# Seven products of squares in place of eight in six blocks of each down projection

## The chip, the cores and the metric

One core of one Trainium2 chip runs the whole program. The metric is the device time of that core in microseconds (us), from launch to end: 571.27 us, the median of 3 runs (571.06 to 572.11). The engines are TensorE (PE, its weight loads PEld), VectorE (DVE), ScalarE (ACT), GpSimd (POOL) and SyncE (SP), which here issues the loads.

## The reference

Two layers of a decoder trunk on 256 tokens of 1024 features, all in float32. Each layer has an attention part (two groups of eight heads, one input and one output projection) and a gated feed-forward part:

```
def hybrid_layer(x, ...):
    ...
    x = x + rms_norm(jnp.einsum('bse,ed->bsd', mix, w_out), g_attn_post)
    h = rms_norm(x, g_ffn_pre)
    f = jax.nn.silu(jnp.einsum('bsd,df->bsf', h, w_gate)) * jnp.einsum('bsd,df->bsf', h, w_up)
    x = x + rms_norm(jnp.einsum('bsf,fd->bsd', f, w_down), g_ffn_post)
```

The down projection `f @ w_down` multiplies 256 x 2816 by 2816 x 1024.

## The kernel before

The weights are cut on the host into blocks of 128 x 2048 float32 (1 MB); a layer has 46, of which the last 11 (`FIRST_DOWN` = 35 on) are the down projection, each 256 rows of `w_down` (two tiles of 128) by all 1024 columns. The tokens are two tiles, t = 0 and 1; a bank of PSUM holds 512 columns of one tile.

A float32 number is split into a high part, rounded to the type that TensorE multiplies, and a low part, the rest. Every product is three matmuls: high by high, high by low, low by high. So a block takes 24 matmuls of 128 x 128 by 128 x 512: two token tiles, eight products of squares (four to a tile), three matmuls each.

A block's way is the same for all. SyncE loads it into one of three slots of `raw` (`load_block`). ScalarE makes the high part `w_h` (`hi`, L559) as soon as the block before it in its slot of `w` (four slots) has been used, VectorE the low part `w_l` (`lo`, L812), and TensorE multiplies (`multiply`, L1209). `freed_by(b)` lists the blocks that may be split once block b has been used; ScalarE and VectorE call `after(L, b)` at places written out by hand, and each engine does its work in exactly that order. A raw slot is loaded again when its low part is done.

The feed-forward part goes by chunks c of 512 of the 2816 inner features (six; the last has 256). Of each chunk and tile ScalarE computes the SiLU of the gate (L671), VectorE multiplies by the up projection (`swiglu`, L1002) and transposes within squares of 32 (`squares_f`, L1013), and GpSimd moves the squares between partitions with 16 copies of 32 partitions (`exchange`, L517): then the features lie along the partitions. ScalarE and VectorE split the result into `fT_h` (`hi_f`, L594) and `fT_l` (`lo_f`, L1020). The chunk's parts are the left operands of the down projection: chunk c feeds the blocks of k = 4c to 4c + 3. GpSimd does this exchange for all six chunks in order, and besides it only sums and powers of one column for the norms (L479 to L505).

TensorE multiplies the first seven down blocks for both tiles, then the last four for tile 0, then for tile 1, with the transposes of the next layer's tile 0 (L1249) put in among the last.

## Time and profile before

| | |
|---|---|
| median of 3 runs | 571.27 us (571.06 to 572.11) |
| profiled execution: span from first to last instruction | 569.7 us |
| between that span and the median of the runs | 1.6 us |
| TensorE busy | 562.0 us, 99% |
| VectorE, ScalarE, GpSimd busy | 375.1, 294.0, 229.1 us |
| read from HBM | 105.72 MB, 187 GB/s over the span |

The profile gives no time of its own for the profiled execution besides its span; the 1.6 us around it are launch and end as the runs' times have them. Busy time of an engine is the time in which it had an instruction under way, and matmuls overlap, so the duration of one (about 390 ns) is longer than the distance from one to the next.

### The profile page before, as it was taken

The numbers are of one execution on the slowest core, as the hardware profiler recorded it, in microseconds if no ns is written. First come the engines' busy times: TensorE is split into PE (matmuls) and PEld (weight loads), VectorE is DVE, ScalarE is ACT, GpSimd is POOL, SyncE is SP. The second block draws the span as 40 slices with busy tenths as digits, with TensorE's granted clock in tenths as the row PEclk, the third lists the DMA queues.
The fourth block names the chain that finished last, engine by engine and source line by source line (L and its number), as shares of the span: only waits on it lengthen the run. The fifth ranks groups of instructions, "written<-read, shape, count | busy, mean of one in ns | idle before, by whom it ended". The sixth has DMA issues, their size and how long they took to land.

```text
span 569.7 us, 8885 instructions
## 1 busy us (share of the span) xinstructions
PE 562.0 (99%) x3395; PEld 462.1 (81%) x3395; DVE 375.1 (66%) x487; ACT 294.0 (52%) x420; POOL 229.1 (40%) x451
## 2 busy tenths in 40 slices
PE   8999999999999999999999999999999999999996
PEld 5878878888888888888888878888888888888884
DVE  5799895946755746365597987775855746734622
ACT  6576684664445353263546748574645354425420
POOL 1101001507797797860120000033296797785000
PEclk9999999999999999999999999999999999999999
DMA  8954624538556461478266443525575455352701
GB/s 299 370 210 156 237 89 173 223 133 315 184 217 202 167 221 33 189 294 298 89 239 208 158 167 124 211 76 221 222 258 201 173 217 183 113 221 88 282 1 74
DMA packets 18730, 107.34 MB, mean 188 GB/s; under 512 B 2816, under 2 KB 3072, under 8 KB 7168
## 3 DMA queue, kind: packets, MB, share of 16 engines
q1 hardware_dynamic: 18688, 106.78, 50.8%
q8 instruction: 27, 0.44, 0.3%
q14 instruction: 15, 0.12, 0.1%
HBM read 105.72 MB, written 1.05 MB: 187 GB/s over the span
## 4 chain that ended last, share of the span: by engine, by line
PE 93%; DVE 3%; DMA 1%; ACT 1%; issue 1%; POOL 0%; SPq 0%; DVEq 0%; POOLq 0%
PE bank L1209 84%; PE bank L1249 4%; PE bank L1234 2%; PE bank L1275 2%; PE bank L1302 2%; DVE w_l L812 1%; DMA raw<-in_w_blocks 1%; ACT work L631 0%; DVE work L896 0%; DVE work L874 0%; DVE work L897 0%; DVE work L952 0%; DVE work L902 0%; DVE x L986 0%; ACT work L608 0%
## 5 line engine op out<-in xcount | busy, mean ns | idle before, releaser
L812 DVE TENSOR_TENSOR w_l<-raw,w_h 128x2048 fp32r<-128x2048 f32 x90 | 206.6, 2301 | 112.6 <-ACT w_h L559 112.4
L559 ACT ACTIVATE w_h<-raw 128x2048 fp32r<-128x2048 f32 x90 | 171.7, 1915 | 108.5 <-PE bank L1209 91.5
L1209 PE MATMUL bank<-w_h,actT_h 128*128 128x512 f32 (+1 forms) x568 | 223.9, 394 | 0.1
L517 POOL COPY work<-work 32x128 f32<-32x128 f32 (+1 forms) x384 | 191.3, 498 | 75.6 <-DVE work L1013 59.8
L1209 PE MATMUL bank<-w_h,actT_l 128*128 128x512 f32 (+1 forms) x568 | 219.9, 387 | 0.0
L1209 PE MATMUL bank<-w_l,actT_h 128*128 128x512 f32 (+1 forms) x568 | 219.4, 386 | 0.0
L1209 PEld LDWEIGHTS bank<-w_h,actT_h 128*128 128x128 f32 x568 | 106.8, 188 | 23.1 <-issue 2.5
L1209 PEld LDWEIGHTS bank<-w_h,actT_l 128*128 128x128 f32 x568 | 106.7, 188 | 22.1
L1209 PEld LDWEIGHTS bank<-w_l,actT_h 128*128 128x128 f32 x568 | 106.9, 188 | 20.1
L504 POOL TENSOR_TENSOR norms<-norms,constants 128x1 f32<-128x1 f32 x8 | 2.7, 342 | 131.7 <-ACT bank L658 131.7
L1209 PE MATMUL bank<-w_h,fT_h 128*128 128x512 f32 x160 | 49.4, 390 | 0.0
L1209 PE MATMUL bank<-w_l,fT_h 128*128 128x512 f32 x160 | 49.3, 389 | 0.0
L1209 PE MATMUL bank<-w_h,fT_l 128*128 128x512 f32 x160 | 49.2, 389 | 0.0
L487 POOL TENSOR_TENSOR norms<-norms,constants 128x1 f32<-128x1 f32 x8 | 6.2, 771 | 72.6 <-ACT work L608 72.6
L1209 PEld LDWEIGHTS bank<-w_l,fT_h 128*128 128x128 f32 x160 | 30.0, 188 | 6.3
L1209 PEld LDWEIGHTS bank<-w_h,fT_l 128*128 128x128 f32 x160 | 30.0, 188 | 6.2
L1209 PEld LDWEIGHTS bank<-w_h,fT_h 128*128 128x128 f32 x160 | 30.0, 188 | 6.2
L1249 PE MATMUL bank<-ident,work 128*128 128x128 f32 x228 | 31.3, 273 | 0.0
L631 ACT ACTIVATE work<-bank,neg_max 128x128 f32<-128x128 f32 (+1 forms) x64 | 26.0, 429 | 10.0 <-DVE neg_max L922 9.9
L1249 PEld LDWEIGHTS bank<-ident,work 128*128 128x128 f32 x228 | 26.9, 140 | 4.7
L671 ACT ACTIVATE work<-bank,norms 128x512 f32<-128x512 f32 (+1 forms) x24 | 15.7, 653 | 28.2 <-PE bank L1209 28.2
L594 ACT ACTIVATE fT_h<-work 128x512 fp32r<-128x512 f32 x20 | 12.5, 624 | 34.3 <-POOL work L517 34.3
(78 smaller groups left out, 396.1 us busy)
## 6 DMA issues: line engine op xcount, KB each, us to landing
raw<-in_w_blocks SPq DMA_DIRECT2D x90, 1024.0 KB, 4.8
bias<-in_b_in SPq DMA_DIRECT2D x8, 256.0 KB, 6.1
raw<-in_w_blocks SPq DMA_DIRECT2D x4, 256.0 KB, 5.9
raw<-in_w_blocks SPq DMA_DIRECT2D x2, 512.0 KB, 8.6
x<-in_x SPq DMA_DIRECT2D x2, 512.0 KB, 10.7
gain_b<-in_g_attn_post SPq DMA_DIRECT2D x2, 512.0 KB, 7.3
bias<-in_g_ffn_pre SPq DMA_DIRECT2D x2, 512.0 KB, 7.4
...
```

The costliest lines, as they stand in the source:

```text
L487: add = nc.gpsimd.tensor_tensor(ss_y[:, t, 0:1], ss_y[:, t, 0:1], eps, ALU.add)
L517: ins = nc.gpsimd.tensor_copy(crossed[t][32 * j:32 * j + 32, i * n:(i + 1) * n], squares[t][32 * i:32 * i + 32, j * n:(j + 1) * n])
L559: nc.scalar.activation(w["h"][:, slot(b), :], raw[:, r, :], ACT.Copy).then_inc(hi_ready, 1)
L594: nc.scalar.activation(f_part("h", c, t), f_view(c, t), ACT.Copy).then_inc(f_hi_ready, 1)
L631: last = nc.scalar.activation(probs[g, r][:, j, n * keys:(n + 1) * keys], bank[b][:, n * keys:(n + 1) * keys], ACT.Exp, bias=neg_max[:, g, ...
L671: nc.scalar.activation(silu[t][:, 0:n], bank[b][:, 0:n], ACT.Silu, scale=rstd_x[:, t:t + 1]).then_inc(drained[b] if c < LAST else last_sil ...
L812: nc.vector.tensor_tensor(w["l"][:, slot(b), :], raw[:, slot(b, RAW), :], w["h"][:, slot(b), :].bitcast(F32), ALU.subtract).then_inc(lo_re ...
L1209: ins = nc.tensor.matmul(bank[BANK_OF[name]][:, 0:n], left[s][:, at + k, tokens(t)], right[r][:, k, c * BANK:c * BANK + n], start=first an ...
L1234: ins = nc.tensor.matmul(bank[BANK_OF[name]][:, 0:n], actT[s][:, k, tokens(t)], right[r][:, k, :], start=first, stop=last and (s, r) == pr ...
L1249: ins = nc.tensor.transpose(out_[:, q * P:(q + 1) * P], src(q), ident[:])
L1275: ins = nc.tensor.matmul(bank[b][:, n * keys:(n + 1) * keys], qT[g][side, i, tokens(t)], kT[g][side, i if g == MOBA else 0, 0:keys], start ...
L1302: ins = nc.tensor.matmul(bank[b][rows, h * HEAD:(h + 1) * HEAD], probsT[g, r][:, j, at + side * 32:at + (side + 1) * 32], v[g][:, kb, cols ...
```

## The change

In six of the eleven down blocks (k = 0 to 11) the 2 x 2 squares of the left operand (two token tiles by two feature tiles, a11 to a22) and of the weights (b11 to b22) are multiplied by a form of Strassen's scheme: seven products in place of eight, each of three matmuls as before. Four products use sums of left squares (s1 to s4), four use sums of weight squares (t1 to t4). VectorE makes the s from the exchanged features, once for each of the first three chunks (`add_s`), and the two engines split them (`hi_s`, `lo_s`). GpSimd makes the t from the raw block with three instructions of 1024, 512 and 512 columns (`add_squares`). A square is thus two entries in the list of blocks: "raw", of which three quarters are split and used, and "sum", split from GpSimd's result and not loaded. Four PSUM banks hold products (M1, M6, M5, M7), and VectorE combines them into the four output banks (`join_first`, `join_second`) with eight additions of 512 columns, in part before TensorE adds the last blocks to the same banks.

The order changes with it: block k = 12 first, then the six squares, then k = 14, 16, 18, 20. GpSimd does the exchange of chunks 4 and 5 after the six sums, where it did them directly after chunk 3 before. The slot order is new (the place at which the raw slots skip is load 26, not block 38), and several buffers share memory.

```diff
@@ -56,9 +56,21 @@
 BLOCKS += [("both", k, 4, LAST * BANK, BANK) for k in (0, 4)]
 FIRST_DOWN = len(BLOCKS)
 KF = FF // P
...
+FAST = 6
+FAST_CHUNKS = FAST // 2
+BLOCKS += [("down", 2 * FAST, 2, 0, D)]
+for k in range(0, 2 * FAST, 2):
+    BLOCKS += [("raw", k, 2, 0, D), ("sum", k, 2, 0, D)]
+BLOCKS += [("down", k, 2, 0, D) for k in range(2 * FAST + 2, KF, 2)]
 NB = len(BLOCKS)
+FIRST_RAW = FIRST_DOWN + 1
+FIRST_LATE = FIRST_RAW + 2 * FAST
+LOADED = [b for b in range(NB) if BLOCKS[b][0] != "sum"]
+NL = len(LOADED)
 PROJ_COLS = [(4 * GROUP, 256), (3 * GROUP, BANK), (GROUP, BANK), (0, BANK), (2 * GROUP, BANK)]
...
+def slot(b):
+    return b % SLOTS
+def before(b):
+    return b - SLOTS
+def raw_slot(b):
+    n = LOADED.index(b)
+    return n % RAW if n < SKIP_AT else (n - NL) % RAW
+def raw_before(b):
+    n = LOADED.index(b) - 1
+    while raw_slot(LOADED[n]) != raw_slot(b):
+        n -= 1
+    return LOADED[n]
...
+        sums_own = sb("sums_own", [P, 2, 2 * BANK])
+        fX = {s: sb("fX_" + s, [P, 10, P], F32R) for s in "hl"}
+        sums = [sums_own[:], gains[:].rearrange("p (a n) -> p a n", a=2),
+                work_row[:, 0:4 * BANK].rearrange("p (a n) -> p a n", a=2)]
+        m1_sum = rope_tmp
+        u4, u2, u3, u7 = (work[:, q, :] for q in (0, 2, 3, 2))
+        s_raw = work_row[:, 0:2 * BANK].rearrange("p (s k n) -> p s k n", s=4, k=2)
         ident = sb("ident", [P, P])
         masks = sb("masks", [P, 4, P], BF16)
...
-                    place_free(lo_ready, L * NB + before(b, RAW) + 1)
-                sp.dma_start(raw[:, r, :], w_blocks[L, b]).then_inc(raw_in[r], 16)
+                    past_L, past = (L, raw_before(b)) if raw_before(b) < b else (L - 1, raw_before(b))
+                    place_free(lo_ready, past_L * NB + past + 1)
+                    if BLOCKS[past][0] == "raw":
+                        place_free(sums_ready, sums_done(past_L, BLOCKS[past][1] // 2))
+                sp.dma_start(raw[:, r, :], w_blocks[L, LOADED.index(b)]).then_inc(raw_in[r], 16)
...
+            def add_squares(L, n):
+                b = FIRST_RAW + 2 * n
+                r = raw_slot(b)
+                dst = sums_of(n)
+                b12, b11, b22, b21 = (raw[:, r, q * BANK:(q + 1) * BANK] for q in range(4))
+                pool.wait_ge(raw_in[r], RAW_IN[r].done(L, b) * 16)
+                if n >= SUMS:
+                    pool.wait_ge(lo_ready, L * NB + b + 2 - 2 * SUMS)
+                if n == 2:
+                    pool.wait_ge(s_lo_ready, FAST_CHUNKS * (L + 1))
+                    pool.wait_ge(drained[BANK_OF["both", LAST, 1]],
+                                 HELD[BANK_OF["both", LAST, 1]].done(L, ("both", LAST, 1)) + 1)
+                nc.gpsimd.tensor_tensor(dst[:, 0, :].rearrange("p (a n) -> p a n", a=2),
+                                        raw[:, r, BANK:3 * BANK].rearrange("p (a n) -> p a n", a=2),
+                                        b12.unsqueeze(1).broadcast_to([P, 2, BANK]), ALU.subtract
+                                        ).then_inc(sums_step, 1)
+                pool.wait_ge(sums_step, 2 * (L * FAST + n) + 1)
+                nc.gpsimd.tensor_tensor(dst[:, 1, 0:BANK], dst[:, 0, BANK:2 * BANK], b11, ALU.add).then_inc(sums_step, 1)
+                pool.wait_ge(sums_step, 2 * (L * FAST + n) + 2)
+                nc.gpsimd.tensor_tensor(dst[:, 1, BANK:2 * BANK], b21, dst[:, 1, 0:BANK], ALU.subtract
+                                        ).then_inc(sums_ready, 1)
...
+                    for t in range(T):
+                        exchange(L, c, t)
+                pool.wait_ge(crossed_in[T - 1], f_count(L, FFN_CHUNKS - 3))
+                for n in range(FAST):
+                    add_squares(L, n)
+                    pool.wait_ge(sums_ready, sums_done(L, n))
+                for c in (FFN_CHUNKS - 2, FFN_CHUNKS - 1):
                     for t in range(T):
                         exchange(L, c, t)
                 rms_y(L, 1, 0)
...
                     act.wait_ge(block_used, USED.done(L, last % NB) + (USED.n if last >= 0 else 0))
-                nc.scalar.activation(w["h"][:, slot(b), :], raw[:, r, :], ACT.Copy).then_inc(hi_ready, 1)
+                if m == "sum":
+                    nc.scalar.activation(w["h"][:, slot(b), :].rearrange("p (a n) -> p a n", a=2), sums_of(k0 // 2),
+                                         ACT.Copy).then_inc(hi_ready, 1)
+                else:
+                    at = BANK if m == "raw" else 0
+                    nc.scalar.activation(w["h"][:, slot(b), at:], raw[:, r, at:], ACT.Copy).then_inc(hi_ready, 1)
             def hi_early(b, p):
...
+            def hi_s(L, c):
+                act.wait_ge(s_added, FAST_CHUNKS * L + c + 1)
+                nc.scalar.activation(s_tiles("h", c), s_raw.rearrange("p s k n -> p (s k) n"), ACT.Copy
+                                     ).then_inc(s_hi_ready, 1)
+            def keep_m1(L):
+                act.wait_ge(block_used, USED.done(L, FIRST_LATE - 2) + USED.n)
+                nc.scalar.activation(m1_sum, products[0][:], ACT.Copy).then_inc(m1_kept, 1)
...
@@ -771,14 +901,18 @@
                         after(L, b + 2)
                         hi_f(L, c - 1, 0)
                         hi_f(L, c - 1, 1)
+                        if c <= FAST_CHUNKS:
+                            hi_s(L, c - 1)
                         after(L, b + 3)
-                hi_f(L, FFN_CHUNKS - 2, 0)
+                for b in range(FIRST_DOWN, NB - 4):
+                    if b == FIRST_LATE - 2:
+                        keep_m1(L)
+                    after(L, b)
+                    if b == NB - 8:
+                        hi_f(L, FFN_CHUNKS - 2, 0)
                 hi_f(L, FFN_CHUNKS - 2, 1)
-                for b in range(FIRST_DOWN, NB - 4):
-                    after(L, b)
-                    if b == FIRST_DOWN + 4:
-                        hi_f(L, FFN_CHUNKS - 1, 0)
-                        hi_f(L, FFN_CHUNKS - 1, 1)
+                hi_f(L, FFN_CHUNKS - 1, 0)
+                hi_f(L, FFN_CHUNKS - 1, 1)
                 sum_y(L, 1, 0)
                 if L < depth - 1:
                     hi(L + 1, 0)
...
-                nc.vector.tensor_tensor(w["l"][:, slot(b), :], raw[:, slot(b, RAW), :],
-                                        w["h"][:, slot(b), :].bitcast(F32), ALU.subtract).then_inc(lo_ready, 1)
+                m, k0 = BLOCKS[b][0:2]
+                if m == "sum":
+                    low, high = (w[s][:, slot(b), :].rearrange("p (a n) -> p a n", a=2) for s in "lh")
+                    nc.vector.tensor_tensor(low, sums_of(k0 // 2), high.bitcast(F32), ALU.subtract
+                                            ).then_inc(lo_ready, 1)
+                else:
+                    at = BANK if m == "raw" else 0
+                    nc.vector.tensor_tensor(w["l"][:, slot(b), at:], raw[:, raw_slot(b), at:],
+                                            w["h"][:, slot(b), at:].bitcast(F32), ALU.subtract).then_inc(lo_ready, 1)
             def after(L, b):
                 for c in freed_by(b):
...
+            def add_s(L, c):
+                for t in range(T):
+                    dve.wait_ge(crossed_in[t], f_count(L, c))
+                if L or c:
...
+                s1, s3, s2, s4 = (s_raw[:, q].rearrange("p k (i b) -> p k i b", b=32) for q in range(4))
+                a11, a12 = f_odd(c, 0, 0), f_odd(c, 0, 1)
+                a21, a22 = f_odd(c, 1, 0), f_odd(c, 1, 1)
+                nc.vector.tensor_tensor(s3, a11, a21, ALU.subtract)
+                link(L, nc.vector.tensor_tensor(s1, a21, a22, ALU.add))
+                link(L, nc.vector.tensor_tensor(s2, s1, a11, ALU.subtract))
+                nc.vector.tensor_tensor(s4, a12, s2, ALU.subtract).then_inc(s_added, 1)
+            def lo_s(L, c):
+                dve.wait_ge(s_hi_ready, FAST_CHUNKS * L + c + 1)
+                nc.vector.tensor_tensor(s_tiles("l", c), s_raw.rearrange("p s k n -> p (s k) n"),
+                                        s_tiles("h", c).bitcast(F32), ALU.subtract).then_inc(s_lo_ready, 1)
+            def join(L, t, c, what):
+                x = bank[BANK_OF["down", t, c]]
+                nc.vector.tensor_tensor(x[:], x[:], what, ALU.add).then_inc(joined, 1)
+            def join_first(L):
...
+                _, m6, m5, _ = products
+                dve.wait_ge(m1_kept, L + 1)
+                join(L, 0, 0, m1_sum)
+                dve.wait_ge(products_full, 3 * L + 1)
+                link(L, nc.vector.tensor_tensor(u2, m1_sum, m6[:], ALU.add))
+                dve.wait_ge(products_full, 3 * L + 2)
+                link(L, nc.vector.tensor_tensor(u4, u2, m5[:], ALU.subtract))
+                join(L, 0, 1, u4)
+            def join_second(L):
+                _, _, m5, m7 = products
+                dve.wait_ge(products_full, 3 * L + 3)
+                link(L, nc.vector.tensor_tensor(u3, u2, m7[:], ALU.add))
+                dve.wait_ge(second_begun, L + 1)
+                join(L, 1, 0, u3)
+                link(L, nc.vector.tensor_tensor(u7, u3, m5[:], ALU.subtract))
+                join(L, 1, 1, u7)
             nc.vector.memset(still, 0.0).then_inc(still_ready, 1)
             dve.wait_ge(xT_in_done[0], 16)
@@ -1125,6 +1312,8 @@
                     for q in range(b + 1, end):
                         after(L, q)
                     if c < FFN_CHUNKS - 1:
+                        if c <= FAST_CHUNKS:
+                            add_s(L, c - 1)
                         lo_f(L, c - 1, 0)
                         lo_f(L, c - 1, 1)
                     swiglu(L, c, 0)
@@ -1134,14 +1323,21 @@
                     after(L, end)
                     if c < FFN_CHUNKS - 1:
                         squares_f(L, c, 1)
-                for t in range(T):
-                    lo_f(L, FFN_CHUNKS - 2, t)
-                    squares_f(L, FFN_CHUNKS - 1, t)
-                for b in range(FIRST_DOWN, NB - 4):
+                    if c <= FAST_CHUNKS:
+                        lo_s(L, c - 1)
+                for b in range(FIRST_DOWN, NB - 7):
                     after(L, b)
-                    if b == FIRST_DOWN + 4:
-                        lo_f(L, FFN_CHUNKS - 1, 0)
-                        lo_f(L, FFN_CHUNKS - 1, 1)
+                lo_f(L, FFN_CHUNKS - 2, 0)
+                squares_f(L, FFN_CHUNKS - 1, 0)
+                join_first(L)
+                after(L, NB - 7)
+                after(L, NB - 6)
+                lo_f(L, FFN_CHUNKS - 2, 1)
+                squares_f(L, FFN_CHUNKS - 1, 1)
+                after(L, NB - 5)
+                lo_f(L, FFN_CHUNKS - 1, 0)
+                join_second(L)
+                lo_f(L, FFN_CHUNKS - 1, 1)
                 scale_y(L, 1, 0)
                 update_x(L, 1, 0)
                 if L < depth - 1:
...
+            def product(out_, left, right, first, last):
+                for s, r in (("h", "h"), ("h", "l"), ("l", "h")):
+                    ins = nc.tensor.matmul(out_[:], left[s], right[r], start=first and (s, r) == ("h", "h"),
+                                           stop=last and (s, r) == ("l", "h"))
+                return ins
+            def squares(L, n):
+                c, k = n // 2, n % 2
+                b = FIRST_RAW + 2 * n
+                first, last = n == 0, n == FAST - 1
+                m1, m6, m5, m7 = products
+                x11, x12, x21 = (bank[BANK_OF["down", t, q]] for t, q in ((0, 0), (0, 1), (1, 0)))
+                a11, a12 = ({s: f_tiles(s, c, 0)[:, 2 * k + u, :] for s in "hl"} for u in range(2))
+                a22 = {s: f_tiles(s, c, 1)[:, k, :] for s in "hl"}
+                s1, s3, s2, s4 = ({s: s_tiles(s, c)[:, 2 * q + k, :] for s in "hl"} for q in range(4))
+                b11, b22, b21 = ({s: w[s][:, slot(b), q * BANK:(q + 1) * BANK] for s in "hl"} for q in range(1, 4))
+                t1, t3, t2, t4 = ({s: w[s][:, slot(b + 1), q * BANK:(q + 1) * BANK] for s in "hl"} for q in range(4))
+                pe.wait_ge(f_lo_ready, F_PARTS.done(L, (c, 1)))
+                pe.wait_ge(s_lo_ready, FAST_CHUNKS * L + c + 1)
+                pe.wait_ge(lo_ready, L * NB + b + 1)
+                product(m1, a11, b11, first, last)
+                product(x12, s4, b22, False, last)
+                product(x11, a12, b21, False, last).then_inc(block_used, 1)
+                USED.tick(b)
+                pe.wait_ge(lo_ready, L * NB + b + 2)
+                ends = [product(m6, s2, t2, first, last), product(m5, s1, t1, first, last),
+                        product(m7, s3, t3, first, last)]
+                if last:
+                    for ins in ends:
+                        ins.then_inc(products_full, 1)
+                product(x21, a22, t4, False, last).then_inc(block_used, 1)
+                USED.tick(b + 1)
             def early(b, t, p, *products, last=False):
...
-                f_landed(L, FFN_CHUNKS - 3)
-                for b in range(FIRST_DOWN, NB - 4):
-                    multiply(L, 0, b)
-                    multiply(L, 1, b)
-                f_landed(L, FFN_CHUNKS - 1)
-                for b in range(NB - 4, NB):
-                    multiply(L, 0, b)
-                for b in range(NB - 4, NB):
-                    if b == NB - 2:
-                        if L < depth - 1:
-                            rows(L + 1, 0, 0)
-                    multiply(L, 1, b)
+                f_landed(L, FFN_CHUNKS - 3, T - 1)
+                multiply(L, 0, FIRST_DOWN)
+                multiply(L, 1, FIRST_DOWN)
+                for n in range(FAST):
+                    squares(L, n)
+                multiply(L, 1, FIRST_LATE, (0,), asks=True).then_inc(second_begun, 1)
+                multiply(L, 0, FIRST_LATE, asks=False, apart=True)
+                f_landed(L, FFN_CHUNKS - 2, 0)
+                multiply(L, 0, FIRST_LATE + 1)
+                multiply(L, 0, FIRST_LATE + 2)
+                f_landed(L, FFN_CHUNKS - 1, 0)
+                multiply(L, 0, FIRST_LATE + 3)
+                pe.wait_ge(joined, 4 * L + 4)
+                multiply(L, 1, FIRST_LATE, (1,))
+                multiply(L, 1, FIRST_LATE + 1)
+                multiply(L, 1, FIRST_LATE + 2, (0,))
+                if L < depth - 1:
+                    rows(L + 1, 0, 0)
+                multiply(L, 1, FIRST_LATE + 2, (1,))
+                f_landed(L, FFN_CHUNKS - 1, 1)
+                multiply(L, 1, FIRST_LATE + 3)
```

`f_tiles` and `s_tiles` say where the split features and their sums lie; `USED`, `LOADED` and the semaphores count as before.

## Rows read from the trace of the kernel before

**Rows 1.** The page's busy line and its clock line, 40 slices.
```profile
PE 562.0 (99%) x3395; PEld 462.1 (81%) x3395; DVE 375.1 (66%) x487; ACT 294.0 (52%) x420; POOL 229.1 (40%) x451
PEclk9999999999999999999999999999999999999999
```

**Rows 2.** The chain that ended last: start, length, what.
```profile
114.64 165.94 PE bank L1209 x732
...
392.83 170.03 PE bank L1209 x750
```

**Rows 3.** Line L1209: durations, first and last start.
```profile
L1209 PEld LDWEIGHTS bank<-w_h,fT_h x160: 187/188/192, 225.8 to 560.0; 128*128 128x128 f32 x160
```

**Rows 4.** Groups by line: busy, mean ns of one.
```profile
L812 DVE TENSOR_TENSOR w_l<-raw,w_h 128x2048 fp32r<-128x2048 f32 x90 | 206.6, 2301 | 112.6 <-ACT w_h L559 112.4
...
L559 ACT ACTIVATE w_h<-raw 128x2048 fp32r<-128x2048 f32 x90 | 171.7, 1915 | 108.5 <-PE bank L1209 91.5 <-DMA raw<-in_w_blocks 17.1
...
L1020 DVE TENSOR_TENSOR fT_l<-work,fT_h 128x512 fp32r<-128x512 f32 x20 | 14.5, 725 | 18.6 <-ACT fT_h L594 18.6
...
L594 ACT ACTIVATE fT_h<-work 128x512 fp32r<-128x512 f32 x20 | 12.5, 624 | 34.3 <-POOL work L517 34.3
```

**Rows 5.** GpSimd's copies: line L517, then its timeline, idle time in brackets.
```profile
L517 POOL COPY work<-work x384: 226/287/2433, 130.7 to 521.9; 32x128 f32<-32x128 f32 x160, 32x64 f32<-32x64 f32 x32
...
197.41 18.95 POOL L517 COPY work<-work 32x128 f32<-32x128 f32 x32 [3.39 <-DVE work L1013]
...
274.58 0.19 POOL L487 TENSOR_TENSOR norms<-norms,constants 128x1 f32<-128x1 f32 x1 [22.82 <-ACT work L608]
...
479.47 13.12 POOL L517 COPY work<-work 32x128 f32<-32x128 f32 x22
```

**Rows 6.** Busy time in stretches; the last row GpSimd's copies alone.
```profile
core 0: us, PE busy (x) PEld busy (x) DVE busy (x) ACT busy (x) POOL busy (x), PEclk, DMA share, GB/s
241.50:244.50 3.00, 3.00 (x15) 2.49 (x14) 0.00 (x0) 1.91 (x2) 2.52 (x11) 1.00 0.63 205
246.00:251.00 5.00, 5.00 (x24) 4.14 (x23) 5.00 (x3) 2.13 (x2) 4.92 (x3) 1.00 0.52 203
...
226.00:229.50 3.50, 3.07 (x11) 1.00 0.97 321
```

**Rows 7.** GpSimd's one-column instructions, and VectorE beside them: line L479, then timelines.
```profile
L479 POOL TENSOR_TENSOR norms<-norms,constants x8: 190/1259/2247, 19.8 to 389.7; 128x1 f32<-128x1 f32 x8
...
111.50 2.25 POOL L479 TENSOR_TENSOR norms<-norms,constants 128x1 f32<-128x1 f32 x1 [3.10 <-ACT work L599]
...
111.42 2.29 DVE L812 TENSOR_TENSOR w_l<-raw,w_h 128x2048 fp32r<-128x2048 f32 x1
...
280.99 1.26 POOL L479 TENSOR_TENSOR norms<-norms,constants 128x1 f32<-128x1 f32 x1 [4.16 <-ACT work L599]
282.32 0.55 POOL L481 TENSOR_TENSOR norms<-norms,constants 128x1 f32<-128x1 f32 x1
...
279.90 2.29 DVE L812 TENSOR_TENSOR w_l<-raw,w_h 128x2048 fp32r<-128x2048 f32 x1 [0.43 <-ACT w_h L559]
282.11 1.28 DVE L842 TENSOR_TENSOR actT_l<-bank,actT_h 128x512 fp32r<-128x512 f32 x2
```

**Rows 8.** VectorE's timeline from chunk 3 into the down projection.
```profile
179.26 2.39 DVE L812 TENSOR_TENSOR w_l<-raw,w_h 128x2048 fp32r<-128x2048 f32 x1 [1.25 <-ACT w_h L559]
...
194.72 0.69 DVE L1020 TENSOR_TENSOR fT_l<-work,fT_h 128x512 fp32r<-128x512 f32 x1 [1.52 <-ACT fT_h L594]
...
201.02 2.29 DVE L812 TENSOR_TENSOR w_l<-raw,w_h 128x2048 fp32r<-128x2048 f32 x1 [0.88 <-ACT w_h L559]
...
211.90 2.29 DVE L812 TENSOR_TENSOR w_l<-raw,w_h 128x2048 fp32r<-128x2048 f32 x1 [2.63 <-ACT w_h L559]
...
244.54 6.85 DVE L812 TENSOR_TENSOR w_l<-raw,w_h 128x2048 fp32r<-128x2048 f32 x3 [3.15 <-ACT w_h L559]
```

**Rows 9.** DMA issues: out<-in, KB each, us to landing.
```profile
raw<-in_w_blocks SPq DMA_DIRECT2D x90, 1024.0 KB, 4.8
```

142 lines of the change are left out of this document (89 added, 53 removed).

## Prediction

> **What bounds the kernel now.** I read the page's busy line and clock first, then the chain of waits, then the engines' timelines around the first down projection, then the rows in which GpSimd and VectorE run at once. TensorE is busy for 562.0 of 569.7 us at the full granted clock [rows 1], and the chain of waits is the matmuls of L1209 nearly throughout. Two pieces of it hold both feed-forward parts: 165.94 us for 732 matmuls and 170.03 us for 750, so 0.2267 us each and no wait between [rows 2]. The durations of 0.39 us in the groups are pipelined and are no price. The down projection of layer 0 starts at 225.8 [rows 3]. A block of 24 matmuls is 24 x 0.2267 = 5.44 us; beside it ScalarE makes one high part (1.915 us) and VectorE one low part (2.30 us) [rows 4], so both have slack.
>
> The resource that matters here shows elsewhere. GpSimd's 32x64 copy takes 0.226 us at the shortest, and in the same group one takes 2.433 [rows 5]. From 246 to 251 us VectorE is busy all 5.00 us with low parts and GpSimd completes 3 copies in that time; in 241.5 to 244.5, with VectorE idle, it does 11 in 3 us [rows 6]. It is no matter of copies: the TENSOR_TENSOR of L479 on one column takes 0.190 us at best, but 2.25 when it starts at 111.50 beside a low part of 111.42 (2.29), and 1.26 at 280.99, ending with the low part that began at 279.90 [rows 7]. L481 at 282.32 keeps its 0.55 us beside L842 of 282.11, one of whose inputs is in PSUM [rows 7]. So a VectorE instruction with two SBUF inputs keeps GpSimd out until it ends.
>
> **What the change takes away.** Six blocks take 7 products of 3 matmuls in place of 8: 21 x 0.2267 = 4.76 us, 0.68 less. Six blocks, two layers: 36 matmuls, -8.16 us, -4.08 a layer. That is all the gain there can be.
>
> **What it adds, per square.** VectorE: low part of 1536 columns, and of 2048 for the sums. From 512 columns at 0.69 to 0.73 and 2048 at 2.29 [rows 4, 8] a column costs 1.04 ns: 1.76 + 2.29 = 4.05 us in place of 2.29. ScalarE the same way: 1.48 + 1.92 = 3.40; both would fit in 4.76 by themselves. GpSimd: three sums of 1024, 512 and 512 columns, which no row shows. Its copies give 0.17 us of launch and 0.95 ns a column (0.226 for 64 columns, 3.07/11 = 0.28 to 0.287, the median, for 128) [rows 5, 6]. Lower bound: a sum costs what a copy does, 3 x 0.17 + 2048 x 0.95 ns = 2.45 us. Upper bound: two operands and the result each take the copy's time, 6.35 us. I take two operands read one after the other, 4.4 us, since a copy differs from a sum by one operand more.
>
> The rows show only that VectorE keeps GpSimd out. I take it both ways, because something that one engine holds to the end of its instruction is most plainly a lock, and so the two times add up: 4.4 + 4.05 = 8.45 us a square, less 0.45 for three launches that run while the other engine moves data (short copies slip between three low parts, 6.85 us in all, without lengthening them [rows 8]). 8.0 us against TensorE's 4.76: the sums become the bound, 3.24 us a square over.
>
> The Trainium skill (GPSIMD Engine Reference, section on performance versus the Vector engine) gives 4497 ns for one add of 2048 fp32 columns; with two launches more my sum by that price would be some 619 us. No run here shows it.
>
> **How far ahead GpSimd is.** It can begin when the exchange of chunk 3 ends, 216.4 now (197.41 + 18.95) [rows 5]. VectorE gets four additions of 256 columns (about 0.43 each) and a low part of 1024 (1.22) per early chunk, all with two SBUF inputs: near 3 us, which also lock out that chunk's copies. TensorE does not feel them: low parts are finished 11.6 us ahead (that of the block multiplied from 225.8 ended at 214.2 [rows 8]). But chunk 3's exchange ends later, at about 221.8. The first sum is then ready near 226.7, its low part near 232.4, and TensorE wants it at 225.8 + 5.44 + 2.04 = 233.3: the first square passes. Three low parts fall into the second sum (1.76, 2.29 and 1.76, less overlap), so it is ready near 236.1 and, with its high part (1.92) and low part (2.29), usable at 240.4; TensorE wants it at 236.0 + 2.04: 2.4 us late. The next four follow at 8.0 us, 3.2 to 3.3 late each. Together 15.5 us; the sixth sum is ready at 236.1 + 4 x 8.0 = 268.1, and TensorE ends the squares at 275.3.
>
> The loads are no cause: a raw block lands 4.8 us after issue [rows 9] and is wanted once in 8 us. It is now also held by the sums, which come before the next load is due.
>
> **What is queued behind.** The exchanges of chunks 4 and 5, which were done at 251.8 (274.58 less 22.82 of idle time, [rows 5]), well ahead of the blocks that need them, now stand behind the sixth sum. The 16 copies of (4,0) are 5.1 us alone and wait for two low parts: 277.2. ScalarE's copy of M1 stands behind the high part of that chunk and one more block, and VectorE's first join behind that: 277.2 + 0.7 + 1.9 + 0.6 + 0.7 = 281.2 with the handovers, while TensorE, done with half a late block at 276.7, waits 4.5 us. The second join (two PSUM additions of 0.7) costs 0.8, the low part behind it 0.9. (5,0) follows (4,1) and waits for three low parts; it ends at 293.3 and is split by 294.3, with TensorE there at 291.1: 3.2. The last joins 0.2. Together 9.7 us. The joins themselves read PSUM, lock nobody out, and else lie under TensorE's four late blocks.
>
> Sum: 15.5 + 9.7 - 4.1 = +21.1 us a layer, and the same in the other layer, where chunk 3's exchange (ended 492.6 [rows 5]) is 10.4 us ahead of the down projection (264 matmuls before 562.86 [rows 2], 503.0), against 9.4 here. +42.2. The smaller buffers, slots moved from block 38 to 26 and the renamed regions I cost at nothing: a load that now waits for the neighbouring block's low part still leaves 11.6 + 5.4 - 4.8 - 1.9 - 2.3 = 8 us. The queue to the next layer is unchanged but for 18 matmuls instead of 24 behind the transposes, 1.4 us of cover less, which the new pace of low parts hides. Made against the profiled span of 569.7, with 1.6 us around it to the median of 571.3: **613.5 us**.
>
> **Rivals.**
> *Only GpSimd waits.* It waits to start while VectorE's instruction runs, but once it has the data path a long sum does not hold VectorE. Rows cannot exclude it: copies are too short, and low parts beside them read 2.29 and 2.39 [rows 8]. Then a square takes about 7.1 us (4.4 and what is left of a low part at each of three starts); the tail stays. +15.1 a layer, 601.5; at copy price +5.6, 582.5. The Trainium skill (SBUF — State Buffer, section on who interferes with whom) says the other: an exclusive lock for whoever starts first, "the other **fully blocks**". The rows agree in one direction; by that rule the forecast stands.
> *Sums at the copy's price*, both waiting: 2.45 + 4.05 is still over 4.76. Squares lose little (about 5 us), the exchanges still come late: +10.5 a layer, 592.3.
> *Sums at the upper price*: 32.8 a layer, 637. Gaps of 3 to 5 us in TensorE's work might also bring its lower clock, which this trace never shows after the start; that would end near here too.
> *Faster.* The sums run beside the low parts. It decides at one place: whether GpSimd's three sums end within 4.76 us while VectorE works 4.05 of them. For it: GpSimd is idle for 22.8 us from 251.8 on [rows 5], and TensorE has not waited once in the part. If sums of [128 x 512] share the memory path as single columns do not, TensorE waits only for joins, 0.4 us a layer: -3.7, that is 563.9. Against it stand all of rows 6 and 7.
> A change that does less than it says is excluded by the count of products, 21 in the code of a square.
>
> **Chances.** Forecast 0.48; only GpSimd waits 0.17; copy price 0.10; upper price or clock 0.10; faster 0.13; within 0.2% 0.02, by a cancellation nobody can plan. 0.2% (1.1 us) is about what a measurement of this kernel tells from no change. Range 578 to 632: it takes in the forecast with the larger part of the way to the upper price, the one-sided wait at both prices and the copy's price (582.5 the lowest); faster (0.13) and the upper price itself stay out. Slower 0.85.
>
> **What would show it.** TensorE idle before the sums' half of each square from the second on, released by VectorE's low part, which waited for ScalarE, which waited for GpSimd. GpSimd's first sum (1024 columns) near 2.1 us alone and 3 or more beside a low part; low parts of 2048 columns stretched beyond 2.29 where a sum had begun (not so if only GpSimd waits). A wait of 4 to 5 us before the first joined bank, one of 3 before the last block of tile 0. Wrong if the low parts and the sums lie side by side at 2.29 and 2 us with TensorE unbroken, or if GpSimd's rows for 512 columns are under 0.5 us.

## The result: 627.3 us, slower by a tenth

The changed kernel takes 627.33 us (median of 4 runs, 626.9 to 629.22) beside 571.16 for the kernel before in the same session: a ratio of 1.0987, interval 1.097 to 1.1005. The forecast was 613.5, slower; the time lies in its range, 14 us above its middle.

First the page of the changed kernel: the busy line, the clock line, and the chain that ended last, by engine.

```profile
PE 572.4 (92%) x3359; PEld 463.9 (74%) x3359; DVE 448.1 (72%) x545; ACT 315.3 (50%) x440; POOL 336.3 (54%) x487
...
PEclk9999999999999978988899999999999999699889
...
POOL 46%; PE 36%; DVE 9%; issue 5%; ACT 2%; DVEq 0%; POOLq 0%; ACTq 0%
```

The chain went by TensorE nearly throughout [rows 2]; now GpSimd has 46% of it. The span is 625.2 against 569.7: +55.5. TensorE runs 36 instructions fewer and is busy 10.4 us longer than in [rows 1]; its idle time grew from 7.7 to 52.8 us. Part of the added busy time is a lower clock: the clock line, flat in [rows 1], now dips several times in each of the two down projections.

GpSimd's timeline in the first down projection (start, length, what; L614, L619 and L621 are the three sums of a square, L597 the exchange's copies; the sums are named by the buffer that they go to, `sums_own`, `gains` and `work` in turn):

```profile
222.56 2.41 POOL L614 TENSOR_TENSOR sums_own<-raw 128x1024 f32<-128x1024 f32 x1
...
226.72 1.26 POOL L621 TENSOR_TENSOR sums_own<-raw,sums_own 128x512 f32<-128x512 f32 x1
228.06 3.75 POOL L614 TENSOR_TENSOR gains<-raw 128x1024 f32<-128x1024 f32 x1
231.89 3.19 POOL L619 TENSOR_TENSOR gains<-gains,raw 128x512 f32<-128x512 f32 x1
235.16 2.68 POOL L621 TENSOR_TENSOR gains<-raw,gains 128x512 f32<-128x512 f32 x1
237.92 2.40 POOL L614 TENSOR_TENSOR work<-raw 128x1024 f32<-128x1024 f32 x1
240.39 1.29 POOL L619 TENSOR_TENSOR work<-work,raw 128x512 f32<-128x512 f32 x1
241.76 1.30 POOL L621 TENSOR_TENSOR work<-raw,work 128x512 f32<-128x512 f32 x1
...
269.31 2.67 POOL L621 TENSOR_TENSOR work<-raw,work 128x512 f32<-128x512 f32 x1
272.04 28.09 POOL L597 COPY work<-work 32x128 f32<-32x128 f32 x56
```

VectorE's timeline beside it (L953 the low part of a raw block, L949 that of a sum block, L1143 `swiglu`):

```profile
227.38 2.21 DVE L953 TENSOR_TENSOR w_l<-raw,w_h 128x1536 fp32r<-128x1536 f32 x1
...
230.15 3.81 DVE L949 TENSOR_TENSOR w_l<-sums_own,w_h 128x2048 fp32r<-128x2048 f32 x1
233.88 0.86 DVE L1143 SCALAR_TENSOR_TENSOR work<-bank,norms,work 128x256 f32<-128x256 f32 x2
234.67 2.03 DVE L953 TENSOR_TENSOR w_l<-raw,w_h 128x1536 fp32r<-128x1536 f32 x1
243.94 3.75 DVE L949 TENSOR_TENSOR w_l<-gains,w_h 128x2048 fp32r<-128x2048 f32 x1 [7.24 <-ACT w_h L674]
...
253.68 3.95 DVE L953 TENSOR_TENSOR w_l<-raw,w_h 128x1536 fp32r<-128x1536 f32 x1
...
273.96 2.29 DVE L949 TENSOR_TENSOR w_l<-work,w_h 128x2048 fp32r<-128x2048 f32 x1 [3.11 <-ACT w_h L674]
```

Read the two together, by their ends. GpSimd's sum of 3.75 us begins at 228.06. VectorE's low part before it ends at 229.59, and from there the sum takes 2.22. VectorE's low part of 3.81 begins at 230.15; that sum ends at 231.81, and from there the low part takes 2.15. GpSimd's 3.19 begins at 231.89 and ends 1.12 after that low part. Each takes about its own length from the moment at which the other ends, by turns and in both directions. The lengths alone are about 2.41, 1.27 and 1.27 us for the three sums (2.40, 1.29 and 1.30 from 237.92 on, where VectorE is idle) and 2.29 for the low part (273.96, where GpSimd's short copies run, and [rows 4]).

TensorE's timeline, the matmuls ahead of which it was idle (in brackets: how long, and what ended it), with one matmul of lower clock (269.17):

```profile
234.61 1.19 PE L1408 MATMUL bank<-w_h,fT_h 128*128 128x512 f32 x2 [9.03 <-DVE work L1143]
...
253.81 0.50 PE L1423 MATMUL bank<-w_h,fT_h 128*128 128x512 f32 x1 [0.35 <-DVE w_l L949]
...
257.77 0.47 PE L1423 MATMUL bank<-w_h,fT_h 128*128 128x512 f32 x1 [0.94 <-DVE w_l L953]
...
260.97 0.50 PE L1423 MATMUL bank<-w_h,fT_h 128*128 128x512 f32 x1 [0.91 <-DVE w_l L949]
...
268.14 0.50 PE L1423 MATMUL bank<-w_h,fX_h 128*128 128x512 f32 x1 [2.03 <-DVE w_l L949]
...
269.17 0.63 PE L1423 MATMUL bank<-w_h,fX_h 128*128 128x512 f32 x1
...
276.31 0.50 PE L1423 MATMUL bank<-w_h,fX_h 128*128 128x512 f32 x1 [1.50 <-DVE w_l L949]
...
285.06 0.50 PE L1408 MATMUL bank<-w_h,fT_h 128*128 128x512 f32 x1 [4.38 <-DVE bank L1187]
...
298.74 0.50 PE L1408 MATMUL bank<-w_h,actT_h 128*128 128x512 f32 x1 [3.60 <-DVE actT_l L1161]
...
324.19 0.50 PE L1408 MATMUL bank<-w_h,actT_h 128*128 128x512 f32 x1 [1.04 <-DVE w_l L953]
```

Up to 298.74 that is 22.7 us of waits; the forecast had 25.2, otherwise placed. One it did not have at all: 9.03 us ahead of the first down block. That block adds into the banks of the last chunk's gate and up, and `swiglu`, which empties them (L1143), stands on VectorE behind the low part of 3.81. Two I had: 4.38 for the first join (forecast 4.5) and 3.60 for chunk 5's features (3.2). The sign that I had named, a wait ahead of the sums' half of each square from the second on, shows from the third square on, with 0.35, 0.91, 2.03 and 1.50 us. Layer 0 as a whole is 28.2 us longer, measured at the next layer's first attention scores (307.82 before, 335.99 after), the second layer 27.3.

### The profile page after: what moved, and what is told of

The parts are those of the page before. It is cut to its first block, busy times and chain, and to the rows that moved or that the text cites. A ratio compares the mean times of both kernels' runs of the same rounds, so it can differ in the third digit from the quotient of the medians.

```text
span 625.2 us, 8989 instructions
## 1 busy us (share of the span) xinstructions
PE 572.4 (92%) x3359; PEld 463.9 (74%) x3359; DVE 448.1 (72%) x545; ACT 315.3 (50%) x440; POOL 336.3 (54%) x487
## 4 chain that ended last, share of the span: by engine, by line
POOL 46%; PE 36%; DVE 9%; issue 5%; ACT 2%; DVEq 0%; POOLq 0%; ACTq 0%
POOL work L597 31%; PE bank L1408 27%; PE bank L1485 3%; POOL gains L614 3%; DVE w_l L953 2%; PE bank L1470 2%; POOL work L614 2%; POOL gains L621 2%; POOL gains L619 2%; PE bank L1511 2%; PE bank L1538 2%; POOL sums_own L614 2%; POOL sums_own L619 2%; DVE work L1143 1%; POOL work L619 1%
## 5 line engine op out<-in xcount | busy, mean ns | idle before, releaser
L953 DVE TENSOR_TENSOR w_l<-raw,w_h 128x2048 fp32r<-128x2048 f32 (+1 forms) x90 | 213.0, 2372 | 55.5 <-ACT w_h L678 54.8
L1408 PE MATMUL bank<-w_h,actT_h 128*128 128x512 f32 (+1 forms) x600 | 235.3, 396 | 7.7 <-DVE actT_l L1161 6.7
L597 POOL COPY work<-work 32x128 f32<-32x128 f32 (+1 forms) x384 | 200.9, 523 | 76.9 <-DVE work L1154 60.9
L1408 PE MATMUL bank<-w_h,actT_l 128*128 128x512 f32 (+1 forms) x600 | 231.2, 390 | 0.0
L1408 PE MATMUL bank<-w_l,actT_h 128*128 128x512 f32 (+1 forms) x600 | 230.6, 389 | 0.0
L678 ACT ACTIVATE w_h<-raw 128x2048 fp32r<-128x2048 f32 (+1 forms) x90 | 165.9, 1855 | 54.6 <-PE bank L1408 35.0
L1408 PEld LDWEIGHTS bank<-w_h,fT_h 128*128 128x128 f32 x32 | 7.9, 254 | 30.1 <-issue 18.6
L949 DVE TENSOR_TENSOR w_l<-gains,w_h 128x2048 fp32r<-128x2048 f32 x4 | 15.4, 3840 | 15.4 <-ACT w_h L674 15.4
L1423 PE MATMUL bank<-w_l,fT_h 128*128 128x512 f32 x64 | 25.0, 391 | 0.0
L1423 PE MATMUL bank<-w_h,fT_l 128*128 128x512 f32 x64 | 25.0, 390 | 0.0
```

What stands on the lines that cost most here:

```text
L597: ins = nc.gpsimd.tensor_copy(crossed[t][32 * j:32 * j + 32, i * n:(i + 1) * n], squares[t][32 * i:32 * i + 32, j * n:(j + 1) * n])
L678: nc.scalar.activation(w["h"][:, slot(b), at:], raw[:, r, at:], ACT.Copy).then_inc(hi_ready, 1)
L949: nc.vector.tensor_tensor(low, sums_of(k0 // 2), high.bitcast(F32), ALU.subtract).then_inc(lo_ready, 1)
L953: nc.vector.tensor_tensor(w["l"][:, slot(b), at:], raw[:, raw_slot(b), at:], w["h"][:, slot(b), at:].bitcast(F32), ALU.subtract).then_inc( ...
L1408: ins = nc.tensor.matmul(bank[BANK_OF[name]][:, 0:n], left[s][:, k, :], right[r][:, k, c * BANK:c * BANK + n], start=first and k == 0 and ...
L1423: ins = nc.tensor.matmul(out_[:], left[s], right[r], start=first and (s, r) == ("h", "h"), stop=last and (s, r) == ("l", "h"))
```

## The experiments

My theory after this: the sums and the low parts exclude each other, and this is the larger part; the late exchanges cost the next; and the 9.03 us are slack, which the sums would have cost anyway. Rivals: the sums are slow in themselves, the banks' wait is on the path, or the lower clock is. Several of these kernels leave out work or put other values in its place, so their output is not the product; each expectation says what.

**Without the sums (no_sums).**

```diff
-                nc.gpsimd.tensor_tensor(dst[:, 1, 0:BANK], dst[:, 0, BANK:2 * BANK], b11, ALU.add).then_inc(sums_step, 1)
...
+                nc.gpsimd.tensor_tensor(junk_sum, eps, minus_half, ALU.add).then_inc(sums_ready, 1)
```

> GpSimd's three sums of a square become one sum of one column; the splits of the 'sum' blocks read the raw block instead of the sums, so the output is not the product (the second operand of four products is wrong) and all other work, its sizes and its order are kept. Theory (the data path shared by GpSimd and VectorE is the bound; the sums fill it): about 40 us vanish, near 585 us; low parts back at 2.29 and 1.76 us, TensorE waits no more inside the squares, and what is left over the kernel before is the wait for the gate products ahead of the first down block and the late exchanges. Rival (the joins, the extra splits and the new order cost most of the 56 us by themselves): above 605 us.

599.33 us (597.84 to 600.82), ratio 1.0487 (1.0455 to 1.0519). Without the sums 28 of the 56 us go; I had expected some 14 us more. In its trace TensorE still waits 5.55 us for the banks of the last chunk, then 2.03 and 3.63 in the tail. That the banks' wait is no longer slack once the sums are gone is tried further down (no_sums_gate_first).

**Low parts that take one input from PSUM (psum_lows).** If the exclusion needs two SBUF inputs, this takes it away in the squares and leaves both engines their work. M7 is added into M5's bank, to free the one that is read, and a sum block's low part becomes two instructions of 1024 columns.

```diff
-                    nc.vector.tensor_tensor(w["l"][:, slot(b), at:], raw[:, raw_slot(b), at:],
-                                            w["h"][:, slot(b), at:].bitcast(F32), ALU.subtract).then_inc(lo_ready, 1)
+                        nc.vector.tensor_tensor(three(w["l"][:, slot(b), at:]), three(raw[:, raw_slot(b), at:]),
+                                                bank[7][:].unsqueeze(1).broadcast_to([P, 3, BANK]), ALU.subtract
+                                                ).then_inc(lo_ready, 1)
```

> GpSimd's sums stay at full size; the low parts of the 'raw' and 'sum' blocks subtract a PSUM bank (broadcast) in place of the high part in SBUF, so VectorE does the same number of columns with only one SBUF input. The values of those low parts are wrong; M5 and M7 share a bank, which frees the one that is read. Theory (exclusion because of two SBUF inputs): the sums go side by side with the low parts, 2.4 + 1.3 + 1.3 = 5.0 us a square, near TensorE's 4.76, and the time falls to about 581 us. Rival (GpSimd's sums are slow by themselves, and VectorE's part in it is small): no more than 10 us are won, above 615 us.

594.82 us (594.47 to 595.16), ratio 1.0408 (1.0387 to 1.0429): 32.5 us less than the changed kernel. GpSimd's timeline of this kernel over the same stretch:

```profile
229.17 2.37 POOL L614 TENSOR_TENSOR gains<-raw 128x1024 f32<-128x1024 f32 x1
231.62 1.28 POOL L619 TENSOR_TENSOR gains<-gains,raw 128x512 f32<-128x512 f32 x1
232.98 1.27 POOL L621 TENSOR_TENSOR gains<-raw,gains 128x512 f32<-128x512 f32 x1
```

and VectorE's:

```profile
231.07 2.35 DVE L950 TENSOR_TENSOR w_l<-sums_own,bank 128x1024 fp32r<-128x1024 f32 x2 [0.25 <-ACT w_h L674]
...
234.12 1.74 DVE L962 TENSOR_TENSOR w_l<-raw,bank 128x1536 fp32r<-128x1536 f32 x1
```

Side by side nothing here is stretched: 2.37 and 2.35 (both halves of the low part together) where it was 3.75 and 3.81. That the sums are slow in themselves (above 615) falls. The 32.5 us are not the sums' alone: this kernel is 4.5 us faster than the one without sums, and the 64 late copies take 28.23 us (from 258.46 on) where they take 33.60 there (from 254.44 on). I had expected some 14 us less than came out. In what is left, 23 us, TensorE waits 7.48 us ahead of the first down block and 3.01 for chunk 5's features, and nowhere within layer 0's squares.

**The gate's work ahead of the squares (gate_first).** The low and high parts of the first square go behind the last chunk's SiLUs and `swiglu`.

```diff
-                    after(L, b)
+                    if c < FFN_CHUNKS - 1:
+                        after(L, b)
...
+                    if c == FFN_CHUNKS - 1:
+                        after(L, b)
```

> ScalarE and VectorE do the gate of the last chunk before they split the first sum block, so the two banks that the first down block writes are free about 5 us earlier; nothing else changes. Theory (the sums on the shared path set the end of the squares, and TensorE's 9 us wait ahead of the down projection is slack behind them): the time stays within 2 us of the changed kernel's 627.3, at most 3 to 5 us less if the lower granted clock (0.59 from 226 to 236 us) cost anything; the wait moves into the squares. Rival (that wait is a cost of its own, the term that my sum lacked): 9 us less in each layer, near 610 us.

627.15 us (626.99 to 628.12), ratio 1.0979 (1.096 to 1.0997): no gain. Three of TensorE's waits in it:

```profile
231.03 1.16 PE L1414 MATMUL bank<-w_h,fT_h 128*128 128x512 f32 x2 [5.00 <-DVE work L1146]
...
259.84 0.50 PE L1429 MATMUL bank<-w_h,fT_h 128*128 128x512 f32 x1 [3.35 <-DVE w_l L952]
...
268.35 0.59 PE L1429 MATMUL bank<-w_h,fX_h 128*128 128x512 f32 x1 [3.35 <-DVE w_l L952]
```

The first wait shrinks by 4.0 us, and 3.9 us come back at the squares: their waits are now 1.42, 3.35, 3.35 and 1.49, in sum 9.6 against 5.7. Two of them are what the forecast had for each (3.2 to 3.3). The sixth square's sum half begins at 276.51 against 276.31: the sums set it. So 4 us of the largest wait in the trace were worth nothing; the 5.00 that stay were not tried by themselves.

**One copy in place of sixteen for the late exchanges (one_copy_late).**

```diff
+                        if c >= FFN_CHUNKS - 2 and (i, j) != (3, 3):
+                            continue
```

> The exchanges of chunks 4 and 5 do one copy in place of 16 (most of these features are not exchanged, so the output is wrong); the sums and all else stay. Theory (these exchanges, queued behind the sixth sum, cost what my sum gave the tail, 9.7 us a layer less the joins, which stay): 14 to 20 us less than 627.3, near 611 us. Rival (the exchanges are hidden behind the sums' delay of TensorE): within 4 us of the changed kernel.

607.04 us (606.54 to 607.55), ratio 1.0622 (1.0601 to 1.0643): 20.3 us back, at the top of what I had expected. The squares' waits stand (2.03 and 1.48 for the last two), those of 4.38 and 3.60 are gone, and one of 0.63 for a late block's low part comes in. The late copies, with the lower clock that follows their waits, cost some 10 us a layer.

**The first join ahead of the features (join_early).** On ScalarE the high part of chunk 4's first features moves back behind the copy of M1, on VectorE its low part behind the joins.

```diff
-                    if b == NB - 8:
+                    if b == FIRST_LATE - 2:
                         hi_f(L, FFN_CHUNKS - 2, 0)
...
                 for b in range(FIRST_DOWN, NB - 7):
                     after(L, b)
+                join_first(L)
                 lo_f(L, FFN_CHUNKS - 2, 0)
                 squares_f(L, FFN_CHUNKS - 1, 0)
-                join_first(L)
```

> ScalarE's copy of M1 goes ahead of the high part of chunk 4's features, and VectorE's first joins ahead of its low part; all work stays. Theory (TensorE's 4.4 us before the first joined bank is order, not work: the copy and the join stand behind an exchange that they do not need): that wait goes, the next one (chunk 4's features) takes half of it back; with the 3.4 us at half clock that follow each of these waits, 4 to 8 us less than 627.3, near 621 us. Rival (the sixth sum and the exchanges behind it set the end whatever is put ahead of them): within 1.5 us of 627.3, since the exchange of (5,0) ends at the same time.

628.56 us (627.86 to 629.41), ratio 1.1001 (1.0982 to 1.1019): the theory (near 621) fell, its rival (within 1.5 us) stood. TensorE's waits of the tail:

```profile
286.06 0.70 PE L1408 MATMUL bank<-w_h,actT_h 128*128 128x512 f32 x2 [2.09 <-DVE w_l L953]
...
299.34 0.80 PE L1408 MATMUL bank<-w_h,actT_h 128*128 128x512 f32 x1 [7.56 <-DVE actT_l L1161]
```

The wait of 4.38 for the join is gone; one of 2.09 for a late block's low part comes in, and 3.60 becomes 7.56. Chunk 5's features let TensorE go on at 299.34 against 298.74 (this trace is already 0.55 later at the first down block), wherever the joins stand: GpSimd's copies of chunk 5's first tile queue behind those of chunk 4 and between the low parts.

**The sums on VectorE (sums_on_vector).** Sums and low parts then stand in one queue and cannot exclude each other. GpSimd is free for the exchanges directly after chunk 3 again, though VectorE's transposes of chunk 5 still come late.

```diff
-                for n in range(FAST):
-                    add_squares(L, n)
-                    pool.wait_ge(sums_ready, sums_done(L, n))
...
             def lo(L, b):
...
+                if m == "raw":
+                    add_squares(L, k0 // 2)
```

> VectorE makes the weight sums itself, just ahead of the low part of the same raw block; GpSimd goes on with the exchanges. Theory (one shared path, used by whoever works): a square costs VectorE 1.76 + 2.29 + 2.3 + launches = 6.7 us instead of 8.25 us on the shared path, still over 4.76: near 600 us, 25 us less than the changed kernel and far slower than before. Rival (GpSimd's rate alone was at fault): VectorE's own sums at half the price would bring it near 575 us.

604.35 us (603.23 to 605.46), ratio 1.0572 (1.0545 to 1.0599), near the 600 of the theory and far from the rival's 575. VectorE's timeline, one square:

```profile
243.37 2.35 DVE L948 TENSOR_TENSOR w_l<-gains,w_h 128x2048 fp32r<-128x2048 f32 x1 [5.22 <-ACT w_h L648]
245.65 1.31 DVE L930 TENSOR_TENSOR work<-raw 128x1024 f32<-128x1024 f32 x1
247.00 0.69 DVE L935 TENSOR_TENSOR work<-work,raw 128x512 f32<-128x512 f32 x1
247.72 0.69 DVE L937 TENSOR_TENSOR work<-raw,work 128x512 f32<-128x512 f32 x1
248.33 1.85 DVE L952 TENSOR_TENSOR w_l<-raw,w_h 128x1536 fp32r<-128x1536 f32 x1
```

The sums cost 2.7 us there and 4.95 on GpSimd, but 2.7 and 4.05 still are over 4.76: six squares in a row outrun VectorE. A share of the sums left to GpSimd would, by these prices and with the exclusion, only add to that; a mixed order was not tried.

**No sums and the gate first (no_sums_gate_first).** The edits of the two kernels together.

> The kernel without sums (sum blocks split from the raw block, output wrong) with the gate of the last chunk ahead of the first sum block's splits. Theory: with the sums gone TensorE's wait ahead of the down projection is no slack any more: of 5.6 us idle and 3.4 us lost to the half clock in each layer more than half comes back, 599.3 falls to about 588 us. Rival (the late exchanges set the end here too): less than 3 us change.

591.79 us (590.37 to 593.21), ratio 1.0352 (1.032 to 1.0385), 7.5 less than no_sums. I had expected about 588; the rival (less than 3 us) falls. So what is slack in the changed kernel is on the path once the sums are out.

**Two squares a layer, sums on VectorE (two_squares).** `FAST = 2`, the sums on VectorE, exchanges right behind chunk 3, the gate first.

```diff
-FAST = 6
+FAST = 2
```

> Two squares in place of six, the sums made by VectorE, the last chunk's gate ahead of the first sum's splits, the exchanges and the features of chunks 4 and 5 in the order of the kernel before; correct output. Theory (seven products pay as long as the sums fit in VectorE's slack ahead of TensorE): 12 matmuls fewer, 2.7 us, and no new wait: 568.5 to 569.5 us against 571.3. Rival (the joins and splits put a wait in front of the joined banks even so): 571 to 575 us.

592.58 us (592.02 to 592.68), ratio 1.0364 (1.0349 to 1.038): wrong by 24 us. ScalarE's timeline says why:

```profile
240.58 0.63 ACT L683 ACTIVATE actT_h<-work 128x512 fp32r<-128x512 f32 x1 [5.19 <-POOL work L593]
241.12 1.89 ACT L644 ACTIVATE w_h<-gains 128x2048 fp32r<-128x2048 f32 x1
```

I had put the split of chunk 4's features ahead of the second sum block's high part. It waits 5.19 us for GpSimd's copies, and the high part with it; TensorE then idles 6.13 us ahead of 245.39. That is a fault of my order, and the expectation had named no queue.

**The same with the split further back (two_squares_b).**

```diff
-                    if b == NB - 8:
+                    if b == FIRST_LATE - 1:
                         hi_f(L, FFN_CHUNKS - 2, 0)
-                hi_f(L, FFN_CHUNKS - 2, 1)
...
+                        hi_f(L, FFN_CHUNKS - 2, 1)
```

> Two squares with VectorE's sums as in the earlier run, but the high and low parts of chunk 4's features go behind the joins (there ScalarE stood at the exchange of chunk 4 with the second sum's splits behind it, and TensorE idled 6.1 us and ran 6.8 us at half clock), and the first sum falls between chunk 4's transposes and the last gate. Correct output. Theory: 592.6 less 12 a layer, 568.5 to 571 us, at or just under the kernel before. Rival (the joins and the gate still wait 1 to 2 us a layer): 571.5 to 575 us.

585.6 us (583.09 to 587.25), ratio 1.0245 (1.022 to 1.0269): 7 us better, still 14 over the kernel before and over both expectations. VectorE's timeline:

```profile
237.70 6.96 DVE L952 TENSOR_TENSOR w_l<-raw,w_h 128x2048 fp32r<-128x2048 f32 x3
244.59 0.69 DVE L1186 TENSOR_TENSOR bank<-bank,work 128x512 f32<-128x512 f32 x1
```

GpSimd's:

```profile
223.89 24.87 POOL L593 COPY work<-work 32x128 f32<-32x128 f32 x30
253.16 8.80 POOL L593 COPY work<-work 32x64 f32<-32x64 f32 x16 [4.40 <-DVE work L1153]
```

And the last of TensorE's waits in the part:

```profile
269.49 0.74 PE L1411 MATMUL bank<-w_h,fT_h 128*128 128x512 f32 x2 [2.78 <-DVE actT_l L1160]
```

The joins stand behind 6.96 us of low parts, and TensorE waits 1.54 and 0.38 us for them. The 30 copies take 24.87 us in place of 0.28 each, beside a VectorE that is hardly idle from 221 to 254; what share of this its sums have was not tried. Chunk 5's features come late (2.78). With the banks' wait of 1.32 that is 6.0 us a layer against 1.4 saved. It names 9 of the 11.6 us by which the profiled run, the fastest of the five, is behind; the rest stays open.

**Work for TensorE in the waits (kept_warm).** 36 and 14 extra matmuls, whose result is not used, into a bank that is started anew afterwards, so that TensorE does not stand.

```diff
+                keep_warm(36, actT["h"][:, 0:2, :])
                 f_landed(L, FFN_CHUNKS - 3, T - 1)
...
+                keep_warm(14, fT["h"][:, 0:4, :])
                 f_landed(L, FFN_CHUNKS - 1, 0)
```

> The changed kernel with matmuls that nobody reads in two of TensorE's waits, into the bank of M1: 36 (8.2 us) ahead of the first down block, where it waits 9.0 us, and 14 (3.2 us) ahead of the last block of tile 0, where it waits 3.6 us. Theory (the half clock after a wait costs time only where TensorE is itself the last to be ready: after the last wait of the tail, not inside the squares): the 10.2 us at half clock in 226 to 241 us vanish and change nothing, those after the last wait (3.4 us) vanish and save 1.7 us a layer: 623.5 to 624.5 us. Rival (the half clock is a main cost of the change, about 10 us a layer): 610 us or less. If the clock does not matter at all: 627.3.

624.93 us (624.5 to 625.42), ratio 1.0938 (1.0922 to 1.0955): 2.4 us less, close to the theory (623.5 to 624.5) and far from the rival's 610. Busy time in stretches (the columns as in [rows 6]), first of the changed kernel:

```profile
226.00:236.00 10.00, 1.39 (x3) 1.16 (x4) 10.00 (x9) 4.01 (x4) 9.69 (x5) 0.59 0.29 107
236.00:241.00 5.00, 5.00 (x19) 4.05 (x18) 0.70 (x1) 0.00 (x0) 4.84 (x3) 0.80 0.35 128
...
301.00:306.00 5.00, 5.00 (x20) 4.04 (x19) 2.98 (x5) 2.85 (x6) 2.07 (x8) 0.82 0.00 0
```

and of this one:

```profile
226.00:236.00 10.00, 9.25 (x41) 7.37 (x40) 10.00 (x9) 4.02 (x4) 9.69 (x5) 1.00 0.30 105
236.00:241.00 5.00, 5.00 (x23) 4.13 (x22) 0.65 (x1) 0.62 (x1) 4.84 (x3) 1.00 0.38 123
...
301.00:306.00 5.00, 5.00 (x24) 4.12 (x23) 3.05 (x5) 3.38 (x6) 2.09 (x8) 1.00 0.01 3
```

The granted clock (the column after POOL) is 1.00 in all three stretches, where it was 0.59, 0.80 and 0.82. Ahead of the squares that buys nothing, since TensorE waits for the same sums a little later (the sixth square's sum half begins at 276.29 against 276.31). Behind 298.74 no sum is left to wait for. In the changed kernel the 36 matmuls from there to the next layer's transposes took 9.92 us in place of 8.16, and here the transposes come 1.06 us earlier, after a new wait of 0.38. The same in both layers would be 2.1 of the 2.4.

**Everything named taken out (remainder).** no_sums, one_copy_late and gate_first in one.

> No sums, one copy in each late exchange, the last chunk's gate first: what is left of the change is seven products, the splits of 1536 and 2048 columns, the sums of features, and the joins (the output is not the product). Theory (these lie in the slack of their engines, but for the gate that waits for chunk 3's later exchange and a short wait at the joins): 572 to 576 us, within 1% of before. Rival (splits or joins cost as such, 6 us or more in a layer): above 583 us.

576.08 us (576.0 to 576.16), ratio 1.0081 (1.0062 to 1.0099), at the upper end of what I had expected. So 51 of 56 us hang on the sums with the low parts, the late copies and the order at the gate. Even without them the 36 matmuls saved show as no gain. In layer 0 TensorE waits 2.85 us at the first down block and 1.07 early in the next layer, and at the lower clock the 24 matmuls from 229.57 on take 7.03 us in place of 5.44. That is 5.5 us against the 4.08 that a layer saves, and 1.4 of the 2.4 us by which this kernel is behind at the next layer's first scores (310.18 against 307.82). No run tried to take these away.

No version of the change beat the kernel before.

## Why the prediction was right, and where it was off

*What bounds, and which way.* Right: the sums become the bound, GpSimd and VectorE add up. The rival *only GpSimd waits* (601.5) falls by the low parts of 2048 columns, which took 3.4 to 4.0 us in place of 2.29. The Trainium skill (SBUF — State Buffer, section on who interferes with whom) has an exclusive lock for whoever starts first; the trace agrees, in both directions.

*The price of the sums.* Mis-sized: "two operands read one after the other, 4.4 us". It is 2.41 + 1.27 + 1.27 = 4.95, a little over 2.2 ns a column. *Copy's price* (2.45) and *upper price* (6.35) fall both. The Trainium skill (GPSIMD Engine Reference, section on performance versus the Vector engine) gives 4497 ns for 2048 columns; an estimate from it, with two launches of 0.17 more, is 4.84, nearer than my term. With 4.95 the forecast's own formula gives the trace: from the second sum's end (237.84) to the sixth's (271.98) GpSimd made four sums and VectorE eight low parts, 4 x (4.95 + 4.05 - 0.45) = 34.2 us, measured 34.1; the forecast had 32.0. The second sum itself ended 1.7 late: the first began 0.8 late, and each took some 0.5 more. Together +3.9 (sixth sum ready 271.98, forecast 268.1), which stands as +4.4 at chunk 5's features (298.74, forecast 294.3).

*The first square passes.* It did, but not for the reason given. Its sum block's low part ended at 233.96 (forecast 232.4), later than the 233.3 at which the forecast has TensorE wanting it; it was in time only because TensorE had not begun. The forecast left out what the first down block claims, the banks that `swiglu` empties, and named nothing queued on VectorE behind the first sum's low part but blocks. gate_first shows that 4 us of this missed wait were worth 0 here; they only moved to the squares. With the sums gone, the same reordering was worth 7.5 us in the two layers.

*The tail.* 4.38 and 3.60 against 4.5 and 3.2: right. Joins took 0.68 to 0.70 each as forecast, high parts 1.48 and 1.92. That one_copy_late gives 10.2 us a layer against 9.7 is in part luck: it keeps the joins, which the 9.7 has in it, and it also gives back lower clock, which the 9.7 has not. (The terms as written, 4.5, 0.8, 0.9, 3.2 and 0.2, make 9.6.) Between the two waits the forecast had 0.8 for the second join and 0.9 for the low part behind it, and the trace has no wait. Instead the 12 matmuls from 285.06 to 289.53 took 4.47 us in place of 2.72, most of them at the lower clock. The second join ended at 287.05, just ahead of the matmul of 287.23 that needs it, so these 1.75 us can be the joins' or the clock's; the trace does not part them.

*The clock.* It was no term of the sum: gaps of 3 to 5 us "might also bring its lower clock" stood only among the rivals, at some 23 us. It came, and cost 1.76 us in layer 0 behind the last wait; kept_warm gave back some 1 us a layer. Ahead of the squares kept_warm removed it without gain.

*Costed at nothing, wrongly.* "1.4 us of cover less, which the new pace of low parts hides": it does not. After the transposes TensorE waits 1.04 us at 324.19 for a low part. The first transposes are 28.24 us later than before (308.66 against 280.42), and the first scores still 28.17, although 6 matmuls (1.36 us) fewer lie between them: 1.3 us lost.

So for layer 0: 21.1 + 4.4 + 1.76 - 0.2 (the last joins, which cost nothing) + 1.3 = 28.4, measured 28.2.

*Faster* (0.13) had one condition, sums within 4.76 us beside 4.05 of low parts. The exclusion denies it. psum_lows also shows that this was not the one place that decides. There the three sums take 4.9 to 5.0 us, hardly over 4.76; the low parts of the sum blocks come every 4.76 us from 244.07 on, TensorE's own pace, and no square waits. It is still 23 us slower than the kernel before, with waits outside the squares.
